# A two-block network on one core: convolutions of the later tiles behind the first solve, in ten row buffers; a tenth expert weight buffer

## The chip, the core and the metric

The kernel runs on one core of a Trainium2 chip. The core has a matmul engine (TensorE, PE in the rows; its weight loads are PEld), an elementwise engine (VectorE, DVE), an activation engine (ScalarE, ACT), GpSimd (POOL) and a queue engine that mostly starts transfers (SyncE, SP). Each executes its own list of instructions in order, and they wait for each other by semaphores. TensorE writes into eight banks of PSUM; everything else lies in SBUF, 128 partitions wide. The metric is the device time of one execution in microseconds.

## The reference, cut to what matters

512 tokens of width 1024 pass through two blocks. The change touches the first one and the seam between them.

```python
# first block
h   = layer_norm(x)
proj = h @ w_in + b_in                       # u,v | q,k,v | z | a,b | gates
qkv = silu(causal_dwconv(dn_qkv, conv_w))    # 24 channel blocks of 128, 4 taps along time
q, k = q / norm(q), k / norm(k)              # per head, 8 heads of 128
amat = I + strict_lower(beta * (k k^T) * decay)
sol  = triangular_solve(amat, [v*beta, k*beta*exp(G)])
o    = recurrence over chunks(sol, q, k)
h1 = layer_norm(ALPHA * h + mix @ w_o)       # mix: gated v-branch and delta-rule branch
# routed experts: 32, each with w1, w3 (1024 x 512) and w2 (512 x 1024), two per token
h2 = layer_norm(ALPHA * h1 + sum_of_two_experts(h1))
# second block: attention, gated recurrence, feed-forward on 16 + 512 tokens
```

All matmuls of the projections are done in two parts for accuracy: every factor is split into a rounded high part and a low part, and three products are summed.

## The kernel before

**Projections.** Work of the first block comes in "dense tiles" ("d", n): 128 output columns by 512 tokens. TensorE does eight steps (k) of two 512-wide matmuls with the high half of the weights, then eight with the low half (`p_dense`). ScalarE makes the high half ahead of time (`s_split_w`, buffers WHU and WHM), VectorE or GpSimd the low half (`low_split_w`, buffers WL). Tiles 0 to 23 are the q, k and v channels, in the order of the list `ORD`. Each of them goes through `s_evac` (ScalarE copies the tile to a row buffer `xps[n % 3]` in ST and scales it into BG), `v_qkv` (three multiply-adds on VectorE, L267, the convolution) and `s_silu` (SiLU, and for q and k a square for the norm). Four squares make one group `r` of sums: `p_sum(r, y, bank)`, four matmuls one column wide (128x1). The groups follow tiles 3 to 9 (r of 0 and 1) or lie inside tiles 18 and 22 (r of 2 and 3).

**Heads.** Tiles 0 to 11 run first (`p_qk` and its counterparts of the other engines). Then `heads` weaves two things on every engine, by a generator that gives one piece of two heads and one piece of the dense work in turn: `p_head`, `v_head`, `s_head`, `g_head` for heads in pairs, and `p_dense1`, `v_dense1`, `s_dense1`, `g_dense1` for tiles 12 to 71. So the order on each engine is fixed by where the `yield`s stand, and an engine that waits in one of the two stands still for both. A head begins with products k k^T and q k^T, masked on VectorE (`LT`, `AT`), then comes the solve of its 16-wide diagonal blocks, for both heads of a pair at once, row by row on VectorE (`v_sub_rows`, L1066 and the tensor-tensor operations around it, `v_sub_spread` last). TensorE then turns the result (tile ("x0", h), L281), and three levels of products complete the inverse (tiles y, xt and xx, with a subtraction on VectorE). At the end of a head its output is scaled by a norm in the next pair's time (`v_tail_sums`, `s_tail` for the root, `v_tail_spread`, `p_tail_scale`, `v_tail`).

**Beta.** `p_beta`, `s_beta` put the scaled betas in rows, SP stores them and spreads them over all partitions (KB); heads can't begin without.

**Experts.** 96 weights of 2 MB go in order into nine buffers (`EXP_SLOTS`); SP starts a load when the buffer's last reader is done (`w_used`) and, for the first round, when what lay in the region has been read (`w_room`). The region H holds h1, 4 x 1024 columns on 128 partitions, all through the experts; it is stored to DRAM (`h1d`) before, from where GpSimd gathers the experts' rows. In `v_meta` VectorE multiplies H by ALPHA, and `p_rows_h` adds it to the result with an identity matrix.

## Time and profile before

| | us |
|---|---|
| median of three runs | 2147.68 (2144.34 to 2149.09) |
| profiled execution, its own time | 2143.43 |
| span of the profile | 2141.5 |
| TensorE busy | 1966.6 |
| VectorE, ScalarE, GpSimd busy | 931.1, 665.3, 443.6 |

The span is the time from the first to the last recorded instruction of one profiled execution; its own time has some 2 us of start and end besides. A row of a timeline has the start, the length, the engine, the line, the operation, what is written and read, and in brackets how long the engine stood idle before it and who released it. "x3" means three instructions in one row, as long as from the first start to the last end. In a row of stretches the granted clock is a share of full speed, 1.00 for 2.4 GHz and 0.50 for 1.2 GHz. A square-sum `p_sum` shows as 128x1 x8.

### The profile page before, as it was taken

The page shows a single profiled execution, that of the slowest core. Times are in us where ns is not written, and L with a number is a line of the kernel's source. Part 1 is how long each engine was busy: PE and PEld are TensorE (multiplying, and loading weights), DVE is VectorE, ACT ScalarE, POOL GpSimd, SP SyncE. Part 2 cuts the span into 40 slices and gives each one's busy share as a digit, 9 for nine tenths or more (in the row PEclk, how much of TensorE's full clock was granted, in tenths as well). Part 3 has the DMA queues.
Part 4 walks back from the last instruction along what each step waited for, and adds up shares of the span by engine and source line. Part 5 has one row for each costly group of instructions (what it writes and reads, how often), then busy time and mean ns, then how long its engine had stood idle before and what let it go on. Part 6 is the DMA issues. An engine that isn't in the chain of part 4 may idle for free.

```text
span 2141.5 us, 23001 instructions
## 1 busy us (share of the span) xinstructions
PE 1966.6 (92%) x9509; PEld 1434.1 (67%) x9509; DVE 931.1 (43%) x1402; ACT 665.3 (31%) x990; POOL 443.6 (21%) x310
## 2 busy tenths in 40 slices
PE   7989999999999889878878799998889999999999
PEld 6768878888777733333333348777667787888887
DVE  6775476643536622111111145445545883222342
ACT  4553432524333101000000133451237753222221
POOL 5542231423325011111111021311003210000121
PEclk9998999999999889999899999999999999999999
DMA  4873443133334589999999963211111134323211
GB/s 166 265 180 69 99 79 79 43 96 79 69 132 177 208 330 409 402 406 409 409 406 411 424 249 122 86 50 50 50 50 40 40 128 157 118 79 113 85 59 40
DMA packets 107782, 367.37 MB, mean 172 GB/s; under 512 B 10666, under 2 KB 43692, under 8 KB 95384
## 3 DMA queue, kind: packets, MB, share of 16 engines
q1 hardware_dynamic: 96928, 341.49, 45.3%
q0 software_dynamic: 8240, 19.00, 2.6%
q10 hardware_dynamic: 2504, 5.35, 0.7%
q8 instruction: 78, 1.28, 0.2%
q14 instruction: 32, 0.26, 0.0%
HBM read 342.94 MB, written 29.15 MB: 174 GB/s over the span
## 4 chain that ended last, share of the span: by engine, by line
PE 77%; DVE 12%; issue 5%; ACT 4%; DMA 1%; POOL 1%; ACTq 0%; SPq 0%; DVEq 0%; POOLq 0%
PE ps L277 72%; PE ps L281 3%; DVE ST L261 2%; PE ps L2151 2%; DVE H L267 1%; ACT ST L273 1%; ACT L273 1%; DVE BG L267 1%; DVE ST L1066 1%; DVE WL L261 1%; ACT M L273 1%; DVE BG L261 0%; DVE ST L1048 0%; DVE ML L261 0%; DVE H L264 0%
## 5 line engine op out<-in xcount | busy, mean ns | idle before, releaser
L277 PE MATMUL ps<-XH,WS 128*128 128x512 f32 x704 | 216.9, 389 | 0.0
L277 PE MATMUL ps<-W,BG 128*64 128x512 f32 x496 | 160.8, 619 | 1.0 <-issue 1.0
L277 PEld LDWEIGHTS ps<-XH,WS 128*128 128x128 f32 x704 | 132.2, 188 | 27.5
L2258 DVE COPY BG<-ps 128x512 f32<-128x512 f32 x32 | 22.1, 692 | 288.0 <-PE ps L277 288.0
L271 ACT ACTIVATE BG<-ps 128x512 f32<-128x512 f32 x48 | 28.6, 595 | 374.9 <-PE ps L2151 339.2
L277 PE MATMUL ps<-XL,WS 128*128 128x512 f32 x352 | 137.0, 389 | 1.4 <-DVE XL L261 1.4
L277 PE MATMUL ps<-X2H,GV 128*128 128x512 f32 (+1 forms) x512 | 127.8, 340 | 0.0
L277 PE MATMUL ps<-M,BG 128*64 128x512 f32 (+1 forms) x304 | 121.6, 544 | 6.4 <-ACT ST L271 6.4
L277 PE MATMUL ps<-ST,BG 128*64 128x512 f32 (+2 forms) x416 | 101.5, 589 | 25.4 <-issue 22.6
L277 PE MATMUL ps<-HTH,WL 128*128 128x512 f32 x448 | 115.1, 394 | 1.4 <-DVE WL L261 1.4
L277 PE MATMUL ps<-BG 128*64 128x512 f32 (+2 forms) x256 | 93.0, 544 | 20.8 <-issue 20.8
L277 PE MATMUL ps<-WS,HH 128*128 128x512 f32 x352 | 108.4, 389 | 0.9 <-DVE WS L261 0.9
L277 PE MATMUL ps<-U,BG 128*64 128x512 f32 x176 | 84.9, 639 | 21.2 <-issue 21.2
L261 POOL TENSOR_TENSOR WS<-W,WS 128x1024 fp32r<-128x1024 f32 x11 | 26.4, 2397 | 362.6 <-ACT WS L271 362.6
L277 PEld LDWEIGHTS ps<-HTH,WL 128*128 128x128 f32 x448 | 85.3, 191 | 20.7 <-DVE WL L261 2.1
L273 ACT ACT_TABLE_LOAD x71 | 91.1, 1283 | 19.6 <-PE ps L277 14.1
L277 PEld LDWEIGHTS ps<-X2H,GV 128*128 128x128 f32 x512 | 88.1, 189 | 10.7
L277 PE MATMUL ps<-X2L,GV 128*128 128x512 f32 (+1 forms) x256 | 87.1, 358 | 6.7 <-DVE H L267 5.4
L261 DVE TENSOR_TENSOR BG<-ps,ST 128x512 f32<-128x512 f32 x22 | 15.2, 692 | 179.1 <-PE ps L277 179.1
L277 PEld LDWEIGHTS ps<-ST,BG 128*64 128x64 f32 (+1 forms) x416 | 40.7, 159 | 77.8 <-issue 74.1
L267 DVE SCALAR_TENSOR_TENSOR BG<-ST,pc,BG 128x512 f32<-128x512 f32 x72 | 73.6, 1023 | 42.7 <-ACT BG L271 40.9
L277 PEld LDWEIGHTS ps<-ST 128*128 128x128 f32 x672 | 85.6, 193 | 7.0 <-DVE ST L261 2.5
(397 smaller groups left out, 4370.5 us busy)
## 6 DMA issues: line engine op xcount, KB each, us to landing
W<-in_w SPq DMA_DIRECT2D x31, 2048.0 KB, 39.3
W<-in_w_in SPq DMA_DIRECT2D x27, 2048.0 KB, 11.0
ST<-in_w SPq DMA_DIRECT2D x21, 2048.0 KB, 35.3
BG<-in_w SPq DMA_DIRECT2D x11, 2048.0 KB, 33.4
U<-in_w SPq DMA_DIRECT2D x11, 2048.0 KB, 32.9
M<-in_w SPq DMA_DIRECT2D x11, 2048.0 KB, 37.9
HT<-in_w SPq DMA_DIRECT2D x11, 2048.0 KB, 39.4
W<-in_w_ffn_in SPq DMA_DIRECT2D x22, 1024.0 KB, 7.7
```

The source lines that it names most:

```text
L261: return E.e.tensor_tensor(o, x, y, op)
L267: return v.e.scalar_tensor_tensor(out=o, in0=x, scalar=c, in1=y, op0=op0, op1=op1)
L271: return s.e.activation(o, x, f, scale=scale)
L273: return s.e.activation(o, x, f, bias=bias, scale=scale)
L277: return p.e.matmul(o, lhsT=l, rhs=r, start=start, stop=stop, skip_group_check=True)
L281: return p.e.transpose(o, x, ident[0:n, 0:n])
L1066: v.e.tensor_reduce(o, z, AX.X, ADD, negate=True).then_inc(v.up())
L2151: z = p.e.transpose(t.at[:, k * BLK:(k + 1) * BLK], xg[j][:, k::8], ident[xg_at[j], xg_at[j]])
L2258: v.e.tensor_copy(hs[j], t.at).then_inc(t.drained)
```

## The change

1. Tiles 14 to 23 get ten row buffers, three in ST and seven in the region H (`HR`), free once h0 is stored; `CONV_AT` names at which tile's turn a convolution is done: those of tiles 14 to 21 in pairs at 19 to 22, so none stands in the first solve.
2. The sums go inside tiles: groups 0 and 1 in tiles 5 and 9 (after k of 1, 3, 5, 7), 2 and 3 in tiles 21 and 23 (3, 5, 7, and 9, which is in the low half).
3. Beta of the first four heads goes to its row after tile 10 instead of 11.
4. The head's scale is done later in the next pair: `v_tail_spread` after the second masks, `v_tail` after the solve's first piece, `p_tail_scale` one piece later.
5. ScalarE splits tile 33 one tile sooner.
6. H becomes the tenth expert buffer; h1 is read back from DRAM behind the last expert weight (`q_h1`), and ALPHA is in the identity that TensorE uses.

```diff
+        Wt += [H.rearrange("p a b -> p (a b)")]
-        EXP_SLOTS = (5, 1, 7, 2, 0, 3, 4, 6, 8)
+        EXP_SLOTS = (5, 1, 7, 2, 0, 3, 4, 6, 8, 9)
...
+        HR = H.rearrange("p i d -> p (i d)")[:, 0:516 * 7]
+        xps += [HR[:, 516 * j:516 * j + 515] for j in range(7)]
+        CONV_AT = {12: [12], 13: [13], 19: [14, 15], 20: [16, 17], 21: [18, 19], 22: [20, 21], 23: [22], 24: [23]}
+
+        def xp_of(n):
+            return n % 3 if n < 12 else (n - 12) % 10
...
+            elif xp_before(n) is None:
+                s.wait_ge(first_done, 3)
             else:
-                s.wait_ge(conv_done, n - 2)
+                s.wait_ge(conv_done, xp_before(n) + 1)
...
-        SUMS_AFTER = {3: [(0, 0)], 4: [(0, 1)], 5: [(0, 2), (0, 3)], 7: [(1, 0)], 8: [(1, 1)], 9: [(1, 2), (1, 3)]}
+        def sums_in(r, bank):
+            return {k: (r, y, bank) for y, k in enumerate((1, 3, 5, 7) if r < 2 else (3, 5, 7, 9))}
...
             tt(v, AT, four(t.at), C, MUL).then_inc(t.drained)
-            if h > 1:
-                v_tail_spread(h - 2)
             yield
...
             v_sub_take(h)
+            if h > 1:
+                v_tail_spread(h - 2)
             yield
-            if h > 1:
-                v_tail(h - 2)
...
                 yield
+                if h > 1 and i0 == 1:
+                    v_tail(h - 2)
...
-                r = {18: 2, 22: 3}.get(n)
+                r = {21: 2, 23: 3}.get(n)
...
-                if n == 30:
-                    s_split_w(32)
+                if n >= 30:
+                    s_split_w(n + 2)
...
-                v_qkv(n)
+                for m in CONV_AT.get(n, ()):
+                    v_qkv(m)
...
-            v.wait_ge(c_h1, 64)
-            for i in range(NT):
-                ts(v, H[:, i, :], H[:, i, :], ALPHA, None, MUL, None).then_inc(alpha_done)
...
-                mm(t.at[:, z], ident, H[:, i, z], stop=False)
+                mm(t.at[:, z], ident_a, H[:, i, z], stop=False)
...
+        def q_h1():
+            for x in w_used[max(n for n in range(N_EXP, N_SEC) if slot[n] == 9)]:
+                q.wait_ge(*x)
+            q.e.dma_start(H, h1d.rearrange("(i p) d -> p i d", p=P)).then_inc(c_h0, 16)
...
+            w_room[N_EXP + EXP_SLOTS.index(9)] = [(c_h1, 64), B["h1", NT - 1, 1].full()]
```

VectorE in the middle of the first pair's solve, before; the operations from ST to ST are rows of the solve, BG<-ST,pc,BG x3 is a tile's convolution.

```order
L261 TENSOR_TENSOR ST<-ST 128x98
L1066 TENSOR_REDUCE ST<-ST 128x2x7
L267 SCALAR_TENSOR_TENSOR BG<-ST,pc,BG 128x512 x3
L261 TENSOR_TENSOR ST<-ST 128x128
L1066 TENSOR_REDUCE ST<-ST 128x2x8
```

And of the change, from the same row of the solve on.

```order
L262 TENSOR_TENSOR ST<-ST 128x98
L1081 TENSOR_REDUCE ST<-ST 128x2x7
L262 TENSOR_TENSOR ST<-ST 128x128
L1081 TENSOR_REDUCE ST<-ST 128x2x8
L262 TENSOR_TENSOR ST<-ST 128x162
L1081 TENSOR_REDUCE ST<-ST 128x2x9
```

Further on in the same list: the last mask of the solve, and what follows it.

```order
L262 TENSOR_TENSOR ST<-lv,ST 128x512
L262 TENSOR_TENSOR WL_52<-W,WHM 128x8x128
L268 SCALAR_TENSOR_TENSOR BG<-ST,pc,BG 128x512 x3
L268 SCALAR_TENSOR_TENSOR BG<-H,pc,BG 128x512 x3
L1300 MEMSET ST 128x8x32
L262 TENSOR_TENSOR ST<-ST,ps 128x16x16
```

The convolutions have left the solve; two of them stand between its last mask and the first level's subtraction, and the second reads its row buffer in H.

TensorE around the end of tile 9, before: the last low half, the row of G, then two sums in one.

```order
L277 MATMUL ps<-HTL,WHU 128x512
L277 MATMUL ps<-HTH,WHU 128x512
L277 MATMUL ps<-HTH,WL_51 128x512 x8
L277 MATMUL ps<-cst,sm 32x128
L277 MATMUL ps<-cst,ST 128x1 x8
```

And of the change, the last two sums of the tile.

```order
L278 MATMUL ps<-cst,ST 128x1 x4
L278 MATMUL ps<-HTL,WHU 128x512
L278 MATMUL ps<-HTH,WHU 128x512
L278 MATMUL ps<-HTL,WHU 128x512
L278 MATMUL ps<-HTH,WHU 128x512
L278 MATMUL ps<-cst,ST 128x1 x4
L278 MATMUL ps<-HTH,WL_51 128x512 x8
L278 MATMUL ps<-cst,sm 32x128
```

All four sums now come ahead of the tile's low half, so the last square is asked for eight matmuls sooner.

SP at the end of the experts' weights, of the change.

```order
L382 DMA HT<-in_w 128x4096
L382 DMA W<-in_w 128x4096
L2662 DMA H<-h1d 128x4x1024
L382 DMA W<-in_w_in 128x8x512 x2
L2667 DMA h0d<-H 128x1024 x4
```

The read of h1 stands between the last expert weight and the second block's first; before, the two loads followed each other directly.

## Rows read from the trace of the kernel before

**Rows 1.** the page, its head and the first part: busy time of TensorE

```profile
span 2141.5 us, 23001 instructions
...
PE 1966.6 (92%) x9509; PEld 1434.1 (67%) x9509; DVE 931.1 (43%) x1402; ACT 665.3 (31%) x990; POOL 443.6 (21%) x310
```

**Rows 2.** stretches: span, TensorE's busy time, granted clock, DMA share, GB/s

```profile
115.00:640.00 525.00, 499.06 (x2708) 0.97 0.38 92
...
760.00:1250.00 490.00, 420.19 (x1924) 0.93 0.99 399
1250.00:2142.00 892.00, 848.46 (x3954) 0.99 0.25 85
```

**Rows 3.** timeline of TensorE; start, length, instructions, [idle before <-releaser]

```profile
95.03 1.87 PE L277 MATMUL ps<-cst,ST 128*128 128x1 f32 x8 [1.54 <-ACT ST L273]
...
123.04 1.16 PE L277 MATMUL ps<-ST,BG 128*128 128x128 f32 x8 [1.74 <-DVE ST L261]
...
157.83 1.87 PE L277 MATMUL ps<-cst,M 128*128 128x1 f32 x8 [6.60 <-ACT BG L271]
...
160.56 1.70 PE L277 MATMUL ps<-cst,M 128*128 128x1 f32 x8
...
174.05 1.04 PE L281 MATMUL ps<-cst,ST 128*128 128x128 f32 x8
```

**Rows 4.** timeline of VectorE through the first solve

```profile
131.48 2.33 DVE L267 SCALAR_TENSOR_TENSOR BG<-ST,pc,BG 128x512 f32<-128x512 f32 x3 [4.84 <-ACT BG L271]
...
139.75 5.09 DVE L267 SCALAR_TENSOR_TENSOR BG<-ST,pc,BG 128x512 f32<-128x512 f32 x3
...
148.07 2.41 DVE L261 TENSOR_TENSOR ST<-ST 128x50 f32<-128x50 f32 x1
...
172.61 0.92 DVE L261 TENSOR_TENSOR ST<-lv,ST 128x512 f32<-128x512 bf16 x1
...
183.92 2.33 DVE L267 SCALAR_TENSOR_TENSOR BG<-ST,pc,BG 128x512 f32<-128x512 f32 x3 [6.21 <-ACT BG L271]
```

**Rows 5.** timeline of GpSimd at 147 us

```profile
147.20 3.21 POOL L261 TENSOR_TENSOR WL<-W,WHU 128x1024 fp32r<-128x1024 f32 x1 [2.91 <-ACT WHU L271]
```

**Rows 6.** timeline of TensorE from 205 us, and the stretch from 210 us

```profile
205.68 0.95 PE L277 MATMUL ps<-cst,M 128*128 128x1 f32 x8
...
211.56 3.38 PE L277 MATMUL ps<-HTH,WL 128*128 128x512 f32 x8
...
222.01 2.00 PE L277 MATMUL ps<-HTH,WL 128*128 128x512 f32 x8
...
210.00:220.00 10.00, 10.00 (x47) 0.77 0.00 0
```

**Rows 7.** timelines of ScalarE and TensorE, second pair of heads

```profile
295.38 1.06 ACT L271 ACTIVATE WHU<-W 128x1024 fp32r<-128x1024 f32 x1 [1.59 <-issue]
...
296.58 0.77 PE L277 MATMUL ps<-HTL,WHU 128*128 128x512 f32 x1 [3.72 <-ACT WHU L271]
```

**Rows 8.** timelines of VectorE and TensorE, third and fourth pair

```profile
403.16 0.18 DVE L1223 RECIPROCAL sm<-sm 128x4 f32<-128x4 f32 x1 [3.66 <-ACT sm L273]
...
433.98 0.66 PE L281 MATMUL ps<-cst,ST 128*128 128x128 f32 x4 [2.46 <-DVE ST L261]
...
556.93 0.66 PE L281 MATMUL ps<-cst,ST 128*128 128x128 f32 x4 [2.86 <-DVE ST L261]
```

**Rows 9.** stretches of 4 us, and the timeline of SP's queue

```profile
764.00:768.00 4.00, 4.00 (x20) 0.99 0.06 20
...
776.00:780.00 4.00, 4.00 (x24) 1.00 0.99 414
...
756.51 12.14 SPq L381 DMA_DIRECT2D ST<-in_w  x2
```

**Rows 10.** stretch of 4 us at the experts' end, and timeline of ScalarE

```profile
1244.00:1248.00 4.00, 3.80 (x20) 1.00 0.40 157
...
1254.08 1.90 ACT L271 ACTIVATE G<-W 128x2048 fp32r<-128x2048 f32 x1
```

More of the change, by code:

```diff
@@ L354, in build @@
         srcs += [w1024(a["w_ffn_out_2"][0], 4 * n, min(4, 22 - 4 * n)) for n in range(6)]
-        EXP_SLOTS = (5, 1, 7, 2, 0, 3, 4, 6, 8)
+        EXP_SLOTS = (5, 1, 7, 2, 0, 3, 4, 6, 8, 9)
         EXP_LAST = (5, 7, 3, 4, 6, 1)
         slot = [n % 2 for n in range(18)] + [0, 1, 2, 0]
-        slot += [EXP_SLOTS[n % 9] for n in range(3 * NE - 6)] + list(EXP_LAST)
+        slot += [EXP_SLOTS[n % 10] for n in range(3 * NE - 6)] + list(EXP_LAST)
         slot += [2, 0, 1, 2] + [(0, 1)[n % 2] for n in range(N_FFI - N_SEC - 4)]
         slot += [(2, 1, 0)[n % 3] for n in range(len(srcs) - N_FFI)]
-        w_sem = [sem(f"weights{i}_loaded") for i in range(9)]
-        w_ready, w_count = [], [0] * 9
+        w_sem = [sem(f"weights{i}_loaded") for i in range(10)]
+        w_ready, w_count = [], [0] * 10
         for n, i in enumerate(slot):
@@ L684, in p_dense @@
                     z = mm(t.at, lo[:, k, :], rhs[0][:, k, :], start=False, stop=k == 7)
+                    if 8 + k in between:
+                        p_sum(*between[8 + k])
             z.then_inc(t.filled)
@@ L718, in build, with xp_before @@
         xps = [XP[:, 516 * j:516 * j + 515] for j in range(3)]
+        HR = H.rearrange("p i d -> p (i d)")[:, 0:516 * 7]
[3 more added lines that the diff above has]
+            return n % 3 if n < 12 else (n - 12) % 10
+        def xp_before(n):
+            return max((m for m in range(n) if xp_of(m) == xp_of(n)), default=None)
         def s_evac(n):
-            t, x = B["d", n], xps[n % 3]
+            t, x = B["d", n], xps[xp_of(n)]
             s.wait_ge(*t.full())
@@ L933, in p_qk @@
             for n in range(12):
-                for _ in first[n] if n < 2 else p_dense(n, n % 4, hTp, "T"):
+                between = sums_in(n // 9, 6 + n // 9) if n in (5, 9) else ()
+                for _ in first[n] if n < 2 else p_dense(n, n % 4, hTp, "T", between):
                     pass
@@ L942, in p_qk @@
                 elif n == 10:
+                    p_beta(1, 6)
                     p_prep3()
-                for r, y in SUMS_AFTER.get(n, ()):
-                    p_sum(r, y, 6 + r)
-            p_beta(1, 6)
         def s_qk():
@@ L973, in v_qk @@
                     v_ab()
+                if n == 10:
+                    v_sums(1)
                 v_qkv(n)
@@ L1128, in p_head @@
                 p_tail_sums(h - 2)
-            yield
-            yield
-            yield
+            for _ in range(4):
+                yield
             if h > 1:
                 p_tail_scale(h - 2)
-            for _ in range(8):
+            for _ in range(7):
                 yield
@@ L1413, in p_dense1 @@
             for n in range(12, 24):
-                r = {18: 2, 22: 3}.get(n)
-                yield from p_dense(n, n % 2, hTp, "T", {k: (r, k - 1, 1) for k in range(1, 5)} if r else ())
+                r = {21: 2, 23: 3}.get(n)
+                yield from p_dense(n, n % 2, hTp, "T", sums_in(r, 0) if r else ())
                 yield
@@ L1509, in s_dense1 @@
                 yield
-                if n == 22:
+                if n == 23:
                     s_sums(3)
                 s_evac(n)
-                s_silu(n - 1)
+                for m in [11] if n == 12 else CONV_AT.get(n - 1, ()):
+                    s_silu(m)
                 yield
-            s_silu(23)
-            s.wait_ge(conv_done, 24)
-            s_row(1, a["gm_ln_g"][0])
-            s_row(2, a["gm_ln_b"][0])
             for n in range(24, 32):
+                if n == 26:
+                    s.wait_ge(conv_done, 24)
+                    s_row(1, a["gm_ln_g"][0])
+                    s_row(2, a["gm_ln_b"][0])
                 if n == 26:
@@ L1524, in s_dense1 @@
                 yield
-                if n == 24:
+                if n == 26:
                     s_beta(3)
+                for m in CONV_AT.get(n - 1, ()):
+                    s_silu(m)
                 m, y = n % 4, (n - 24) // 4
@@ L1589, in v_dense1 @@
                 yield
+                for m in CONV_AT.get(n, ()):
+                    v_qkv(m)
                 m, y = n % 4, (n - 24) // 4
@@ L2222, in s_experts @@
                     s.e.dma_start(ST[:, 16:18, :].rearrange("p a b -> p (a b)"), rope_d).then_inc(c_rp, 16)
+                    act(ident_a, ident, ACT.Copy, scale=ALPHA).then_inc(dg_done)
                     s.wait_ge(dst_done, 1)
@@ L3819, in _ @@
             q_merge()
-            for n in range(21, N_SEC + 2):
+            for n in range(21, N_SEC):
+                q_weight(n)
+            q_h1()
+            for n in range(N_SEC, N_SEC + 2):
                 q_weight(n)
```

35 lines of the change are left out of this document (20 added, 15 removed).

## The prediction, made before the changed kernel was run

> **What bounds the kernel now.** I read the page first: TensorE is busy 92% of the span [rows 1]. Next the waits of TensorE and the stretches, to see where the other 8% lies. From 115 to 640 us (the eight heads of the delta rule, woven with the projections) TensorE is busy 499 of 525 us at a mean granted clock of 0.97; from 760 to 1250 us (the experts) it is busy 420 of 490 us, and there the DMA share is 0.99 at 399 GB/s, so the weights' transfers set the pace; behind 1250 us little is lost and nothing is edited but who scales the residual [rows 2]. So a gain must be a wait of TensorE or low clock before 640 us, or bytes moved earlier in the expert stage. The chain that ended last runs through TensorE almost everywhere in the woven stage, and through VectorE in four places: the triangular solves, one for each pair of heads. Third view, the timelines round those.
>
> In the first solve TensorE stands 6.60 us at 157.83, and the four sums of squares in that tile then run at half clock: 1.70 us each [rows 3] against 0.95 us in a later tile [rows 6]. Its releaser is the square on ScalarE, whose convolution on VectorE stood in line between pieces of the solve. VectorE has no gap there: four convolutions (tiles 14 to 17) lie between 139.75 and 172.61 us, the first of 5.09 us, three of the 2.33 us that one takes undisturbed [rows 4].
>
> **The first solve.** In the new order those four follow the solve. VectorE's path gets shorter by 5.09 + 3 x 2.33 = 12.1 us. It also starts earlier: the row sums' product goes to TensorE one tile sooner, so the spread of beta comes earlier and the 1.74 us wait at 123.04 [rows 3] goes; the solve itself cannot start more than about those 1.7 us earlier, since the convolution of tile 13 (131.48, it waited 4.84 us for ScalarE's copy of that tile) still stands ahead of it [rows 4]. The last mask then begins at 172.61 - 12.1 - 1.7 = 158.8 us. TensorE comes there earlier than that: 174.05 less 6.60, less 1.74, less four slow sums of 1.70 and some 4 us of half clock, is about 155, so it waits for the solve; it turns XT at about 159.0 and not at 174.05. **Term: -15.0 us.** The four sums come back in tile 21: 4 x 0.8 (0.95 us, overlapping its neighbours a little) [rows 6]. **Term: +3.2.** Bounds: -7.5, if only half of it shows, and -17, if GpSimd's collisions (below) miss the solve.
>
> **Clock in tiles 21 to 23.** From 210 to 220 us TensorE is granted 0.77, though it never idles: four sums, each behind only two wide matmuls, and then small half products go before it. Eight wide matmuls take 3.38 us at 211.56 and 2.00 at 222.01 [rows 6]. Counting this group and the two before it, 3.2 us. The new sums have four wide matmuls between them (k of 3, 5, 7, 9), and fewer small ones in any stretch. **Term: -3.2** (bounds 0 and -3.2).
>
> **Tiles 5 to 10.** The sums move inside tiles 5 and 9. In tile 9 this is bad: the square of tile 7 is late (TensorE waited 1.54 us for it at 95.03, with the tile done [rows 3]), and TensorE now meets it ahead of eight wide matmuls (2.0 us) and without the sum that stood before it (0.8): a wait of 1.54 + 2.0 + 0.8 = 4.3 us, of which only the low clock behind it, 1.4 us on eight matmuls, is new loss, since the rest is work that still runs. Tile 5's sums no longer stand in one lump, which may spare as much. I take **0** for all of it, bounds -4 and +4.
>
> **Ten row buffers, tiles 19 to 25.** VectorE now does two convolutions in each of tiles 19 to 22, 4.7 us where 2.3 stood, and ScalarE two SiLUs and squares in a row; ahead of the levels' subtractions in both engines' order. What hides them: their inputs lie ready in ten buffers, so VectorE does them while TensorE runs a tile (24 wide matmuls, 6 us at the pace of rows 6, and the heads' products); before, it stood 6.21 us for the copy of tile 18 [rows 4]. SiLU of tile 23 now falls between two GELUs, with table loads. I take **+1.5**; bounds 0 and, with every one of the six subtractions behind a pair of convolutions, 6 x 4.66 = +28.
>
> **Later solves.** Second pair: the split of tile 33 is issued before ScalarE queues two row loads (it waited 1.59 us for that issue at 295.38), and TensorE's 3.72 us at 296.58 shrink [rows 7]; VectorE's solve is right behind as next limit, and it gains the same 1.6 us, and some 0.9 (a quarter of the 3.66 us that the third pair shows) because the head's scale no longer stands ahead of a mask. **Term: -2.5**, bounds 0 and -6. Third and fourth: VectorE stood 3.66 us at 403.16 for ScalarE's root; TensorE waits 2.46 and 2.86 us at the end of those solves [rows 8]. The scale's work moves behind the first sum of the solve, so the second head's masks fill the gap. But only those masks fit in, two operations at a third of 2.33 us, 1.6 us, and the two spreads still have to be done ahead of the solve's end. **Term: -1 each, -2**; bounds 0 and -7.
>
> **The tenth weight buffer.** SP issues the ninth expert weight at 756.51 and the tenth transfer 12 us later, when the first expert has read its weights; from 764 to 768 us the DMA share is 0.06, while from 776 on it is 0.99 at 414 GB/s [rows 9]. H is free by then (its rows are stored and turned), so a transfer of 2.1 MB, 5.1 us at 410 GB/s, fills the hole. As the stage runs at the DMA's pace from then on, its end comes earlier by what the hole held. **Term: -4.8**, bounds 0 and -5.1. By the Trainium skill (DMA: Bandwidth & Descriptors, Bandwidth) a core reads HBM at about 358 GB/s; the trace does not agree, it shows 399 to 414, and at 358 the hole would hold less than one buffer and the term would still be its 4.5 us.
>
> **What comes in.** H must be read back, 2.1 MB, and it goes ahead of the second block's first weight. Before, the DMA had run dry between 1244 and 1248 us (share 0.40) and the first split of that weight began at 1254.08 [rows 10]. With the experts' end 5 us earlier and 5 us of H added, the weight lands at the same 1246, and is needed at 1249: hidden with some 3 us to spare. The scaling by alpha leaves VectorE, which waited for ScalarE there anyway, and moves into TensorE's identity: same matmuls, one small copy. **0**; bounds 0 and +3.
>
> **Sum:** -15.0 + 3.2 - 3.2 + 0 + 1.5 - 2.5 - 2 - 4.8 = -22.8. The span goes from 2141.5 to 2118.7 us. The profiled execution took 2143.4; the runs' median, 2147.7, is 4.3 above it, and the lowest 2144.3. Taken from the median: 2124.9; since the profiled execution was below all three runs I lean a little under that, **2124.0**.
>
> **Collisions on VectorE.** At 148.07 a sum of 50 elements took 2.41 us, and ended with GpSimd's split (147.20, 3.21 us) [rows 4, 5]; the convolution at 139.75 lost 2.76 us the same way. The Trainium skill (SBUF — State Buffer, section Who interferes with whom) says that a VectorE operation with two SBUF inputs and a GpSimd operation that reads SBUF exclude each other for a whole instruction; by that rule, with which these rows agree, the paired convolutions should meet GpSimd's splits more often. That is the third rival's mechanism.
>
> **Rivals.**
> 1. *The later solves open wholly.* All of 3.72, 2.46 and 2.86 us and some 3 us of low clock behind them go, 12 us where I count 4.5: 2116.5. Against it: VectorE is gapless through those solves.
> 2. *The hole in the DMA isn't worth anything*, because the end of the expert stage is set by something else: the row gathers, or the stand at the meta tokens. 2129. Against it: 0.99 share over the stage.
> 3. *Levels behind paired convolutions.* Two or three of the six subtractions wait the whole 4.66: 12 us back, 2136. Should all six be exposed, with one collision of 2.76 us, 28 + 2.8 - 1.5 come in against a gain of 22.8: 2153, slower than before. It decides from five on: five leave 2146, no change. For it: in-order engines, 4.7 us in one lump. Against it: the 6.21 us that VectorE stood idle there.
> 4. *The first solve stays bound elsewhere* (a weight that lands late for ScalarE's split of tile 20, masks of GpSimd): half of the first term, 2131.5.
>
> **Chances.** Forecast 0.50 (its own range 2119 to 2130), rival 1 0.14, rival 2 0.10, rival 3 in part 0.12, with five exposed 0.04 and whole 0.04, rival 4 0.06. Eight in ten: 2112 to 2138. A measurement of this kernel tells about 0.2% (4.3 us) from no change. Faster 0.92, same 0.04, slower 0.04.
>
> **What would show it.** VectorE's solve of the first pair without convolutions, ended near 159; TensorE's 6.60 us idle gone, a short one of 2 to 3 us before the turn; a new idle of some 4 us in tile 9; clock 1.00 where 0.77 stood; DMA share near 1 from 760 to 768, and the last expert 4 to 5 us closer to the first. Wrong would be: idle of TensorE behind subtractions between 160 and 220, or the second block's first split later than TensorE's end of the experts.

## The result, and the profile after

The changed kernel took 2130.99 us in the median of four runs (2129.22 to 2132.55), the kernel before 2148.39 us beside it (four runs, 2144.34 to 2151.56): a ratio of 0.9934, 95% interval 0.992 to 0.9949. Measured once more beside the last kernels below, it had a ratio of 0.995 (0.9932 to 0.9967). The profiled execution took 2129.22 us, its span is 2127.3: 14.2 us less than before. Forecast were 22.8 us less and a time of 2124.0, in a range of 2112 to 2138. So the direction and the range of eight in ten held, but the median lies 7.0 us above the forecast time, just outside the forecast's own range (2119 to 2130), and by the spans 8.6 us of the forecast gain are missing.

The page of the changed kernel, its head and TensorE's busy time (to be held against [rows 1]):

```profile
span 2127.3 us, 23006 instructions
...
PE 1961.0 (92%) x9509; PEld 1428.6 (67%) x9509; DVE 933.9 (44%) x1398; ACT 669.0 (31%) x994; POOL 441.0 (21%) x311
```

The chain and the shares say little here; the timeline does. A "turn" below is TensorE's transpose of a solved block, the row cst,ST 128x128 x8 (the last of them cst,BG). TensorE in the changed kernel, through the first solve and the levels behind it (beside [rows 3, 6]):

```profile
93.55 1.57 PE L278 MATMUL ps<-cst,ST 128*128 128x1 f32 x8 [3.78 <-ACT ST L274]
...
124.21 3.75 PE L278 MATMUL ps<-ST,BG 128*128 128x128 f32 x16 [2.41 <-DVE ST L262]
...
163.88 2.21 PE L282 MATMUL ps<-cst,ST 128*128 128x128 f32 x8 [3.75 <-DVE ST L262]
...
210.84 1.94 PE L282 MATMUL ps<-cst,BG 128*128 128x128 f32 x16
```

The 6.60 us wait at 157.83 is gone, and XT is turned 10.2 us earlier (174.05, now 163.88). But the wait for beta is still there (2.41 us), and a wait of 3.75 us stands ahead of the turn. Stretches of the same kernel (length, then the busy time of TensorE, its weight loads, VectorE, ScalarE and GpSimd, then granted clock, DMA share and GB/s) show what follows those two waits, and that the low clock of [rows 6] is gone:

```profile
120.00:130.00 10.00, 7.59 (x34) 6.34 (x34) 7.79 (x5) 3.81 (x6) 8.57 (x8) 0.83 1.00 233
160.00:170.00 10.00, 6.25 (x21) 4.88 (x21) 7.20 (x10) 1.71 (x3) 0.51 (x1) 0.66 0.00 2
...
210.00:220.00 10.00, 10.00 (x74) 9.28 (x73) 9.19 (x14) 5.62 (x7) 2.47 (x1) 1.00 0.16 25
```

VectorE in the changed kernel (beside [rows 4]), then GpSimd in the same stretch:

```profile
118.79 3.91 DVE L268 SCALAR_TENSOR_TENSOR BG<-ST,pc,BG 128x512 f32<-128x512 f32 x3 [2.07 <-ACT BG L272]
...
122.62 3.21 DVE L262 TENSOR_TENSOR ST<-BG,KB 128x512 f32<-128x512 f32 x2
...
132.29 2.33 DVE L268 SCALAR_TENSOR_TENSOR BG<-ST,pc,BG 128x512 f32<-128x512 f32 x3 [4.47 <-ACT BG L272]
...
139.61 1.04 DVE L1063 TENSOR_REDUCE ST<-ST 128x64 f32<-128x512 f32 x1
...
144.51 2.12 DVE L262 TENSOR_TENSOR ST<-ST 128x32 f32<-128x32 f32 x1
...
158.42 2.81 DVE L262 TENSOR_TENSOR ST<-ST 128x450 f32<-128x450 f32 x1
...
164.03 0.90 DVE L262 TENSOR_TENSOR ST<-lv,ST 128x512 f32<-128x512 bf16 x1
```

```profile
139.01 2.93 POOL L262 TENSOR_TENSOR WL<-W,WHU 128x1024 fp32r<-128x1024 f32 x1
...
144.20 2.38 POOL L262 TENSOR_TENSOR WL<-W,WHU 128x1024 fp32r<-128x1024 f32 x1
...
158.16 2.35 POOL L262 TENSOR_TENSOR WL<-W,WHM 128x1024 fp32r<-128x1024 f32 x1 [11.58 <-ACT WHM L272]
```

The four convolutions are out of the solve. Its last mask begins at 164.03, where 158.8 was forecast: the convolution ahead of the solve began at 132.29 and not before 131.48 as it should, and products of 32 and 450 elements last 2.1 and 2.8 us beside GpSimd's splits, 0.2 and 1.0 us without them (run pool_free below).

The later pairs of heads, TensorE:

```profile
276.29 1.10 PE L278 MATMUL ps<-ST,cst 128*128 128x512 f32 x2 [1.24 <-DVE ST L262]
...
399.78 1.10 PE L278 MATMUL ps<-ST,cst 128*128 128x512 f32 x2 [1.08 <-DVE ST L262]
403.16 1.10 PE L278 MATMUL ps<-ST,cst 128*128 128x512 f32 x2 [2.29 <-DVE ST L262]
...
527.70 2.04 PE L278 MATMUL ps<-ST,cst 128*128 128x512 f32 x2 [2.28 <-DVE ST L262]
...
549.23 1.04 PE L282 MATMUL ps<-cst,ST 128*128 128x128 f32 x8
```

The waits of 2.46 and 2.86 us ahead of the turns [rows 8] are gone. In their place TensorE waits at the product that spreads the output scale: 6.9 us in four rows.

How far the changed kernel is ahead of the kernel before, at the same instruction of TensorE (start before less start after):

| place | before | after | ahead |
|---|---|---|---|
| first turn of XT, pair 1 | 174.05 | 163.88 | 10.2 |
| second turn | 186.86 | 179.14 | 7.7 |
| third turn (four sums came back ahead of it) | 199.77 | 195.47 | 4.3 |
| turn behind the levels | 219.34 | 210.84 | 8.5 |
| turn, pair 2 | 311.71 | 301.37 | 10.3 |
| turn, pair 3 | 433.98 | 425.04 | 8.9 |
| second turn, pair 4 | 570.37 | 561.95 | 8.4 |
| first expert's transposes | 756.49 | 747.94 | 8.6 |
| router turn in the experts' last part | 1228.68 | 1214.01 | 14.7 |
| second block's transposes | 1287.43 | 1273.10 | 14.3 |

### The profile page after: what moved, and what is told of

It reads as the page before. It is cut to its first block, busy times and chain, and to the rows that moved or that the text cites. A ratio compares the mean times of both kernels' runs of the same rounds, so it can differ in the third digit from the quotient of the medians.

```text
span 2127.3 us, 23006 instructions
## 1 busy us (share of the span) xinstructions
PE 1961.0 (92%) x9509; PEld 1428.6 (67%) x9509; DVE 933.9 (44%) x1398; ACT 669.0 (31%) x994; POOL 441.0 (21%) x311
## 4 chain that ended last, share of the span: by engine, by line
PE 77%; DVE 12%; issue 4%; ACT 4%; DMA 2%; POOL 0%; SPq 0%; DVEq 0%; POOLq 0%; ACTq 0%
PE ps L278 72%; PE ps L282 3%; DVE ST L262 3%; DMA W<-in_w_in 2%; PE ps L2176 1%; ACT ST L274 1%; DVE H L268 1%; ACT L274 1%; ACT M L274 1%; DVE ST L1081 1%; DVE WL L262 1%; DVE BG L262 0%; DVE BG L268 0%; DVE ML L262 0%; DVE ST L1063 0%
## 5 line engine op out<-in xcount | busy, mean ns | idle before, releaser
L278 PE MATMUL ps<-ST,BG 128*64 128x512 f32 (+2 forms) x384 | 137.4, 567 | 8.8 <-issue 5.0
L278 PE MATMUL ps<-M,BG 128*64 128x512 f32 (+1 forms) x288 | 105.1, 545 | 11.5 <-ACT ST L272 6.4
L278 PEld LDWEIGHTS ps<-W,BG 128*64 128x64 f32 x448 | 46.8, 144 | 78.4 <-issue 77.4
L278 PEld LDWEIGHTS ps<-X2H,GV 128*128 128x128 f32 x512 | 89.5, 192 | 10.7
L278 PE MATMUL ps<-H,BG 128*64 128x512 f32 (+1 forms) x256 | 84.6, 525 | 12.6 <-issue 8.3
L272 ACT ACTIVATE WS<-W 128x2048 fp32r<-128x2048 f32 (+1 forms) x44 | 65.3, 1484 | 78.1 <-PE ps L278 64.3
L2303 POOL DMA_INDIRECT BG<-h1d,toki x32 | 30.9, 966 | 277.7 <-PE ps L2176 263.1
```

The lines of the kernel that those rows point to most:

```text
L272: return s.e.activation(o, x, f, scale=scale)
L278: return p.e.matmul(o, lhsT=l, rhs=r, start=start, stop=stop, skip_group_check=True)
L2303: g.e.indirect_dma_start(out=xg[j], out_offset=None, in_=h1d, in_offset=bass.IndirectOffsetOnAxis(ap=toki[:, b:b + 1], axis=0), bounds_che ...
```

## The experiments

Up to 1.8 us of a place in time belongs to the execution: the wait of tile 9 ended between 92.91 and 94.67 us in nine profiles of kernels that are the same up to there. Where less than that matters, I count from that row ("from tile 9"), which does not take all of it away: in five profiles with the same order up to there, the fourth turn comes 115.93 to 117.77 us behind it and the first 69.33 to 70.84 us; "the fourth turn" is the row at 210.84. Each run lies beside the kernel before on its chip.

**Undoing the parts.** Without the tenth buffer:

```
-        EXP_SLOTS = (5, 1, 7, 2, 0, 3, 4, 6, 8, 9)
+        EXP_SLOTS = (5, 1, 7, 2, 0, 3, 4, 6, 8)
...
-            q.e.dma_start(H, h1d.rearrange("(i p) d -> p i d", p=P)).then_inc(c_h0, 16)
+            pass
```

> The changed kernel without the tenth weight buffer: nine buffers for the experts, H not overwritten and so not read back; ALPHA stays in TensorE's identity. Up to the first expert it is the changed kernel (first transposes at 747.9 us). My theory: the expert stage and the seam behind it gave 5.8 us of the 14.2 (first transposes 8.55 us earlier than before, second block's first transposes of M 14.33 earlier), all of it by the buffer that fills the hole in the DMA; the span goes from 2127.3 to about 2133.1, and a stretch of 4 us near 756 shows a DMA share near 0.06 again. Rival 1: part of it is the scaling by alpha that left VectorE at the seam; then the span is 2130 to 2131.5. Rival 2: reading H back costs something at the seam, so without it less is lost: 2131.

Measured: 2135.03 us, ratio 0.995 (0.9934 to 0.9966), which is also the ratio of the changed kernel in its second measurement. But the profiled execution, the fastest of the six, has a span of 2128.6, 1.3 us more than the changed kernel's and not 5.8. The first 20 us of the stage (from 4 us ahead of the first transposes), first the changed kernel, then this one:

```profile
743.94:763.94 20.00, 15.23 (x82) 7.39 (x84) 5.17 (x22) 2.86 (x4) 3.70 (x4) 0.78 0.88 321
```

```profile
742.50:762.50 20.00, 15.22 (x82) 7.36 (x84) 5.14 (x22) 2.86 (x4) 3.68 (x4) 0.78 0.71 236
```

The hole is real: 0.17 of 20 us, 3.4 us of all the DMA engines. My 5.8 us for it was wrong for this profile, and the rivals' 2130 to 2131.5 were too high for it as well; the runs' median does not tell them apart. No run put alpha back on VectorE, so the first rival was not tested by itself. More on it at the end of this section.

With each convolution in its own tile again:

```
-        CONV_AT = {12: [12], 13: [13], 19: [14, 15], 20: [16, 17], 21: [18, 19], 22: [20, 21], 23: [22], 24: [23]}
+        CONV_AT = {n: [n] for n in range(12, 24)}
...
-                r = {21: 2, 23: 3}.get(n)
+                r = {18: 2, 22: 3}.get(n)
```

> The changed kernel with each convolution of tiles 14 to 23 in its own tile again, as before, and the sums of squares that depend on them in tiles 18 and 22 again (with the new spacing inside the tile). My theory: VectorE's path through the first solve gets four convolutions back, 5.0 + 3 x 2.24 = 11.7 us, less what of the 5.5 us of collisions with GpSimd moves away; TensorE turns XT at 173 to 176 us in place of 163.9, the half clock behind that wait stays, and the sums no longer stand in tile 21; at the fourth turn behind the first pair (210.84 us now) the lag is 8 to 10 us, the span 2135 to 2137. Rival: the gain came from the sums' spacing and the clock at 200 to 220 us (4.2 us), not from VectorE's path; then the span is 2131 or less.

Measured: 2138.46 us, ratio 0.996 (0.9946 to 0.9973), span 2136.3. TensorE, and the stretch in which its tile 22 runs:

```profile
156.41 1.38 PE L278 MATMUL ps<-cst,M 128*128 128x1 f32 x8 [4.31 <-ACT BG L272]
...
172.35 1.04 PE L282 MATMUL ps<-cst,ST 128*128 128x128 f32 x8
...
198.04 1.03 PE L282 MATMUL ps<-cst,ST 128*128 128x128 f32 x8
...
214.39 1.80 PE L282 MATMUL ps<-cst,BG 128*128 128x128 f32 x15
```

```profile
205.00:215.00 10.00, 10.00 (x66) 8.92 (x66) 3.96 (x9) 6.78 (x9) 0.38 (x1) 1.00 0.00 1
```

Both theories were half right. At the first turn the move of the convolutions (and of the sums that follow them out of tile 18) is worth 8.5 us (172.35 against 163.88), at the fourth only 3.6 (214.39 against 210.84). The other 5.0 us of the 8.5 that the change has there (219.34 less 214.39) are kept by a kernel whose convolutions lie as before. Of these, 1.7 us are there at the first turn already (174.05 less 172.35), where TensorE waits 4.31 us in place of 6.60. The larger part comes later: from the third to the fourth turn TensorE takes 19.57 us before, 16.35 here, 15.37 in the changed kernel. The same four sums of tile 22 stand in this stretch before and here, only with four wide matmuls between the first and second and between the second and third, where there were two; the last two sums still have two between them, which the prediction had as four. Their spacing is worth 3.2 us, and the granted clock there is 1.00 where it was 0.77 [rows 6].

With the output scale in its old places (TensorE's product one step earlier, VectorE's spread behind the mask of AT, its use ahead of the solve's first sum):

```
+            if h > 1:
+                v_tail_spread(h - 2)
             yield
             v.wait_ge(de_done, 2 * h + 2)
...
             v_sub_take(h)
-            if h > 1:
-                v_tail_spread(h - 2)
```

> The changed kernel with the three edits of the output scale undone (VectorE's spread and scale and TensorE's scale product in their old places in each head). The prediction's theory: the later scale spares VectorE about 1 us in each later solve, so this kernel is slower by 2 to 3 us: 2129 to 2130. My theory now: the later scale left TensorE's product in line ahead of it, which waits 1.24 us at 276.29, 1.08 and 2.29 at 399.78 and 403.16, 2.28 at 527.70; undone, those go and the waits before the turns at 425 and 549 us come back with 1 to 2.9 us each, so that it is even or slightly faster: 2125 to 2127.5. The places tell: of the 1.9 us that the changed kernel lost against before between 311 and 570 us, this one loses none.

Measured: 2135.33 us in the median of five runs (a sixth took 7711.94 us and is left out), ratio 0.994 (0.9926 to 0.9955); span 2135.0. TensorE's turns of pair 3 and 4:

```profile
424.16 0.66 PE L282 MATMUL ps<-cst,ST 128*128 128x128 f32 x4 [2.45 <-DVE ST L262]
...
548.76 2.22 PE L282 MATMUL ps<-cst,ST 128*128 128x128 f32 x8 [2.87 <-DVE ST L262]
...
588.56 1.91 PE L282 MATMUL ps<-cst,BG 128*128 128x128 f32 x16
```

The four waits at the scale are gone and the two ahead of the turns are back, as my theory had it. Between the turn of pair 2 and the row at 588.56 this kernel takes 286.65 us (from 301.91), the changed one 286.05 (301.37 to 587.42): level within 0.6 us. But the kernel before took 284.14 us there (311.71 to 595.85), with the same order and the same waits as this run, 2.46 and 2.86 us. The difference of 2.5 us is the clock behind these waits: from the turn to the next one this run takes 15.04 and 14.32 us, the kernel before 13.43 and 13.44. The stretch behind the turn of pair 3, before and in this run:

```profile
433.90:438.90 5.00, 4.47 (x26) 3.73 (x27) 2.86 (x5) 1.72 (x3) 1.71 (x1) 1.00 0.27 72
```

```profile
424.10:429.10 5.00, 4.49 (x16) 3.62 (x17) 2.85 (x5) 1.72 (x3) 1.42 (x1) 0.66 0.72 90
```

So the scale's move costs 1.9 us against an execution in which the clock stays up behind the old waits, and gains 0.6 us against one in which it falls; what decides between the two is not shown. My 2125 to 2127.5 was wrong. The span is 8 us longer, nearly all of it for reasons behind 588 us: 2.6 more up to the experts, 2.4 in them, 2.2 at their end, where nothing is edited.

With tiles 3 to 11 in their old order (beta's product behind tile 11, sums behind tiles 3, 4, 5, 7, 8, 9):

```
-                between = sums_in(n // 9, 6 + n // 9) if n in (5, 9) else ()
...
+                for r, y in SUMS_AFTER.get(n, ()):
+                    p_sum(r, y, 6 + r)
+            p_beta(1, 6)
```

> The changed kernel with the order of tiles 3 to 11 as before (sums of squares of q and k behind tiles 3, 4, 5, 7, 8 and 9, product of beta behind tile 11, the wait for eG ahead of beta). The prediction's theory: beta earlier takes a wait of 1.7 us away and starts the solve as much earlier, the sums cost nothing; so this kernel is 1.7 us slower, 2129. My theory now: the wait ahead of the second products (2.41 us at 124.21 now, 1.74 + 0.30 before) was only handed from the DMA of beta's rows to a convolution of VectorE that stands in line there, and the 3.78 us at 93.55 are new; without both the solve starts 0.8 us earlier and the span is 2126 to 2127.

Measured: 2129.03 us, ratio 0.9917 (0.9904 to 0.9929), span 2130.8. TensorE:

```profile
93.51 1.62 PE L278 MATMUL ps<-cst,ST 128*128 128x1 f32 x8 [1.52 <-ACT ST L274]
...
121.42 1.16 PE L278 MATMUL ps<-ST,BG 128*128 128x128 f32 x8 [1.65 <-DVE ST L262]
...
162.74 2.22 PE L282 MATMUL ps<-cst,ST 128*128 128x128 f32 x8 [3.63 <-DVE ST L262]
```

The wait in tile 9 is 1.52 us, and at beta there are two, 1.65 and 1.64 us, since VectorE here waits for the DMA of beta's rows before each of its two products. The first turn comes 1.1 us earlier than in the changed kernel and the fourth 0.7 us (210.18), which is less than executions differ by. So the new order of these tiles gains nothing that can be seen; by the prediction this run should have been 1.7 us later. The runs go further: the ratio 0.9917 lies below both of the changed kernel's (0.9934 and 0.995) and its interval clear of the second's. No row up to the fourth turn shows where such a gain would come from, and this run's profiled execution is the slowest of its six; that the old order is faster stays possible and open.

**What holds the first solve.** The convolution of tile 12 behind the products of k and beta:

```
-        CONV_AT = {12: [12], 13: [13], 19: [14, 15], ...
+        CONV_AT = {13: [12, 13], 19: [14, 15], ...
```

> The changed kernel with the convolution of tile 12 one tile later (both of 12 and 13 in tile 13), so that in VectorE's order the products of k and beta of the first two heads stand ahead of it. My theory: the rows of beta have landed by 120 to 121 us (issued 114.1, 5.2 to 6.7 us to landing), and the wait of 2.41 us at 124.21 is due to that convolution (118.79, 3.91 us) alone; it goes, with the half clock behind it (3.75 us for 16 products where 2.3 would do), and the first turn of XT comes at 160 to 161 in place of 163.9; VectorE's second convolution is hidden in the 4.47 us that it stands idle ahead of 132.29. Rival: the DMA is what is late; then the wait stays at 1.5 us or more and the turn at 163 or later.

Measured: 2128.08 us, ratio 0.9922 (0.9893 to 0.9952), span 2127.0. VectorE, then TensorE:

```profile
120.14 0.70 DVE L262 TENSOR_TENSOR ST<-BG,KB 128x512 f32<-128x512 f32 x1 [2.83 <-DMA KB<-b_rows]
```

```profile
123.70 1.16 PE L278 MATMUL ps<-ST,BG 128*128 128x128 f32 x8 [0.23 <-DVE ST L262]
...
161.48 0.91 PE L282 MATMUL ps<-cst,ST 128*128 128x128 f32 x4 [4.52 <-DVE ST L262]
```

The 2.41 us became 0.23. From tile 9 the first turn comes 3.5 us earlier (66.81 us behind 94.67, against 70.33 behind 93.55) and the fourth 4.1 us (113.15 against 117.29). VectorE waits 2.83 us for the landing of beta's rows, which is just early enough for TensorE. TensorE now waits 4.52 us for the solve: it was moved earlier by as much as the solve.

The splits of tiles 18 and 20 on VectorE (`x not in (('d', 18), ('d', 20))` added to the list of GpSimd's splits):

> The changed kernel with the splits of tiles 18 and 20 (GpSimd, 144.20 with 2.38 us and 158.16 with 2.35 us) given to VectorE, 1.22 us each. My theory: in the first solve each cost VectorE 1.9 us by holding up one small operation (2.12 us for 32 elements at 144.51, 2.81 us for 450 at 158.42), so in VectorE's own hands they cost 2 x 0.7 less: the turn of XT comes 1.4 us earlier, at 162.5, with TensorE's wait ahead of it 1.4 us shorter. Rival: the slow ones are not due to GpSimd; then they stay above 2 us at the same elements and the turn comes 2.4 us later, at 166.3.

Measured: 2128.82 us, ratio 0.992 (0.9896 to 0.9945), span 2126.0. The product of 32 elements takes 0.21 us (2.12 before the edit), that of 450 elements 0.98 (2.81), and TensorE, with the stretch round it:

```profile
161.76 0.66 PE L282 MATMUL ps<-cst,ST 128*128 128x128 f32 x4 [1.00 <-DVE ST L262]
```

```profile
160.00:170.00 10.00, 8.55 (x50) 7.00 (x49) 8.82 (x11) 2.57 (x6) 2.80 (x2) 1.00 0.02 8
```

The wait ahead of the turn is 1.00 in place of 3.75 us. From tile 9 the first turn is 2.6 us earlier (1.6 to 3.1 against the five profiles of one order) where 1.4 were expected, and the fourth 4.4 us (112.84): behind a wait of 1.00 us the half clock does not follow, and from the first turn to the second 13.43 us pass where 15.26 did, so the low clock there cost 1.8 us. GpSimd's splits held up VectorE more than the work itself costs there.

Both convolutions, 12 and 13, behind the solve, four in tile 19:

```
-        CONV_AT = {12: [12], 13: [13], 19: [14, 15], 20: [16, 17], ...
+        CONV_AT = {19: [12, 13, 14, 15], 20: [16, 17], ...
```

> The changed kernel with the convolutions of tiles 12 and 13 behind the first solve too (tile 19 takes 12 to 15, tile 20 takes 16 and 17). My theory: what starts the solve on VectorE is the convolution of tile 13 (132.29, it waits 4.47 us for ScalarE's copy); without it the masks and sums of the solve start at 129 to 131 and the turn of XT comes at 156 to 158 in place of 163.9, about when TensorE gets there, without its wait of 3.75 us and without the half clock of the ten us behind it. At the fourth turn (210.84 now) 6 to 9 us are kept. Rival 1: GpSimd's masks and the exponentials of ScalarE set the start of the solve, and it moves no further than in the kernel with convolution 12 alone moved (turn 160 to 161). Rival 2: four convolutions in a lump in tile 19, 9.3 us, hold up the first level's subtraction; then 3 to 5 us of it are lost again before 211.

Measured: 2131.97 us, ratio 0.9938 (0.9919 to 0.9956), span 2134.9. VectorE, TensorE, and one stretch:

```profile
161.42 8.50 DVE L268 SCALAR_TENSOR_TENSOR BG<-ST,pc,BG 128x512 f32<-128x512 f32 x9
169.83 2.32 DVE L268 SCALAR_TENSOR_TENSOR BG<-H,pc,BG 128x512 f32<-128x512 f32 x3
```

```profile
158.22 0.65 PE L282 MATMUL ps<-cst,ST 128*128 128x128 f32 x4 [1.48 <-DVE ST L262]
172.76 1.97 PE L282 MATMUL ps<-cst,ST 128*128 128x128 f32 x8 [2.06 <-DVE ST L262]
```

```profile
190.00:200.00 10.00, 10.00 (x37) 8.83 (x36) 4.62 (x9) 1.67 (x3) 1.95 (x2) 0.50 0.01 2
```

Theory and second rival both came true. The first turn begins at 156.14, 7.7 us earlier, so the convolution of tile 13 does set its start. Then the level's subtraction stands behind 10.7 us of convolutions (the first three read ST and the fourth H, since tiles 12 and 13 share the ten buffers), TensorE waits 2.06 us, again 0.59 and 0.88 us for ScalarE's eight passes behind the lump, and runs ten us at half clock. From the second turn to the third, at 198.05, 25.3 us pass where 16.3 did, and at the fourth turn (213.47) it is behind the changed kernel.

**The output scale still later**, two steps in TensorE's order of a head, `for _ in range(4)` becoming `range(6)`, and its use on VectorE behind the solve's third sum:

> The changed kernel with TensorE's product that spreads the output scale two steps later in each head (and VectorE's use of it behind the second sum of the solve). My theory: the four waits ahead of it (1.24 us at 276.29, 1.08 and 2.29 at 399.78 and 403.16, 2.28 at 527.70, 6.9 us together) go, but VectorE's solves set the turns at 301, 425 and 549 us: of the 6.9 us most comes back as longer waits there, except in the fourth pair, where TensorE had no wait left at its turn. Relative to the turn at 301, the turn at 425 keeps its distance within 0.5 us, with a wait of 2 to 3.5 us ahead of it. Rival: TensorE's own order is the limit, and all 6.9 us are kept: the row at 587.42 comes 6 to 7 us earlier.

Measured: 2134.2 us, ratio 0.9954 (0.9938 to 0.997), span 2130.2. TensorE's turns of pairs 2, 3 and 4:

```profile
300.24 0.66 PE L282 MATMUL ps<-cst,ST 128*128 128x128 f32 x4 [2.44 <-DVE ST L262]
...
424.31 2.23 PE L282 MATMUL ps<-cst,ST 128*128 128x128 f32 x8 [2.86 <-DVE ST L262]
...
548.13 0.66 PE L282 MATMUL ps<-cst,ST 128*128 128x128 f32 x4 [2.79 <-DVE ST L262]
```

The four waits at the scale are gone, and 2.4 to 2.9 us stand ahead of each turn, in the fourth pair too, where I had expected some of it to be kept. The turns of pairs 2 and 3 lie 124.07 us apart, 123.67 in the changed kernel. Wherever the scale's product stands, the solve ends when it ends. Behind the waits of 2.44 and 2.86 us the clock fell (0.66 and 0.69 in the next 5 us), behind that of 2.79 us it did not (1.00).

**Mixtures, and the tenth buffer again.** Three edits together (tile 12's convolution later, the two splits on VectorE, tile 9's last sum among the half products):

> The changed kernel with three edits: the convolution of tile 12 behind the products of k and beta (as in the run with that alone), the splits of tiles 18 and 20 on VectorE (as in the run with those alone), and the last sum of squares inside tile 9 moved from behind the eighth pair of wide matmuls to among the half products (position 13), with row sums 1, 3, 5 as they are. My theory: the 3.78 us at 93.55 shrink to 1.5 or less, the 2.41 us at 124.21 to 0.3, the 3.75 us at the first turn to 1 or 2, and half clock follows none of them; the two gains of 4.1 and 4.4 us at the fourth turn share 2.5 us of clock, so the fourth turn comes 6 to 8 us earlier than the changed kernel's 210.84, at 203 to 205, and the ratio to the kernel before is 0.990 to 0.991. Rival: VectorE, with two splits more and the convolution of tile 12 inside, becomes later at the start of the solve; then the fourth turn is at 206 or later.

Measured: 2124.25 us, ratio 0.9916 (0.9893 to 0.9939), span 2118.9; the fourth turn at 202.66, 8.2 us earlier. The waits at beta are 0.70 and 1.64 us (TensorE now gets there before beta's rows do), the one in tile 9 is 2.39 where 1.5 or less was expected, the one ahead of the turn 2.02, with the clock at 1.00 behind it.

The same, with 12 and 13 in tile 18 behind the solve:

```
-        CONV_AT = {12: [12], 13: [13], 19: [14, 15], ...
+        CONV_AT = {18: [12, 13], 19: [14, 15], ...
...
+                ... {1: (1, 0, 7), 3: (1, 1, 7), 5: (1, 2, 7), 13: (1, 3, 7)} if n == 9 ...
```

> As the kernel of the run with the same splits and sum, but with the convolutions of both tiles 12 and 13 in tile 18, right behind the first solve, and 14 and 15 in tile 19 as in the changed kernel: two in a tile, where the run with four in tile 19 had a lump. My theory: what that run lost (9 us between the third and the second turn, of them 5 us of half clock at 190 to 200 us) came from the lump of four convolutions and eight passes of ScalarE behind it; spread over two tiles it stays away, the solve ends at 153 to 156, TensorE comes to the first turn without a wait of over 0.5 us, and the fourth turn is at 200 to 203; ratio to the kernel before 0.989 to 0.990. Rival: not the lump, but TensorE that now comes early to the levels is what waits: then the waits before 200 us come back in the other places, 3 us or more, and the fourth turn is at 205 or later.

Measured: 2124.09 us, ratio 0.9905 (0.9888 to 0.9922), span 2123.8. TensorE:

```profile
155.32 1.04 PE L282 MATMUL ps<-cst,ST 128*128 128x128 f32 x8
168.77 1.21 PE L282 MATMUL ps<-cst,ST 128*128 128x128 f32 x8 [0.59 <-DVE ST L262]
...
200.66 1.94 PE L282 MATMUL ps<-cst,BG 128*128 128x128 f32 x16
```

No wait is left ahead of the first turn, and the fourth is at 200.66, 10.2 us earlier than in the changed kernel. Two convolutions in a tile are hidden but for a wait of 0.59 us, four are not: it was the lump.

> The kernel above without the tenth weight buffer (nine buffers, H not read back). The profiles so far disagree on its worth: first expert's transposes to the combined rows took 466.1, 468.4, 469.5, 468.3, 468.8, 467.8, 465.9 and 469.5 us with the buffer and 472.2 and 469.0 without. My theory: the buffer is worth the 4.8 us of the prediction or less, 2 to 4 us, as the executions of the stage differ by 3 us themselves; here the median is 2 to 4 us longer than that of the kernel with the buffer. Rival: it is worth the 6.2 us that the first pair of profiles showed; then 5 to 7 us longer.

Measured: 2125.12 us, ratio 0.9914 (0.9896 to 0.9932), span 2121.8. That is 1.0 us over its twin with the buffer, where 2 to 4 were expected, and less than this measurement can tell.

> The changed kernel once more, beside the others on the same chip, so that the two mixed kernels have it to be compared with: span 2127 to 2131, ratio 0.992 to 0.995. Its places in time before 700 us repeat within 1.2 us (an offset that is there before 95 us), its stretch through the experts within 3 us.

Measured: 2132.48 us, ratio 0.995 (0.9932 to 0.9967), span 2130.6, fourth turn 211.09. Beside it mix_b is 8.4 us shorter, and 21 us shorter than the kernel before (2145.28): the kernel that beats both.

With 14 profiles the tenth buffer can be read by stage. From the first expert's transposes to the router turn near 1214 us, eleven profiles with the buffer take 468.0 us in the mean (465.9 to 469.5), three without it 470.9 (469.0 to 472.2): 2.9 us less. From there to the second block's transposes eleven take 59.5 us (57.6 to 61.3), three 58.4 (57.6 to 58.9): 1.1 us more. The ranges touch or overlap and there are only three profiles without it, so both differences are rough, the second above all. The first pair of profiles, 14.7 less 8.6 us, had paired a slow execution of this stage with a fast one. GpSimd's last two stores of expert rows, first without the buffer, then with it (the changed kernel again):

```profile
1235.55 0.98 POOL L2264 DMA_INDIRECT ypad<-BG,yrow  x1 [10.13 <-DVE BG L2275]
...
1241.00 0.98 POOL L2264 DMA_INDIRECT ypad<-BG,yrow  x1 [2.44 <-DVE BG L2275]
```

```profile
1235.21 0.98 POOL L2265 DMA_INDIRECT ypad<-BG,yrow  x1 [10.13 <-DVE BG L2276]
...
1241.91 0.98 POOL L2265 DMA_INDIRECT ypad<-BG,yrow  x1 [0.80 <-DMA ypad<-BG,yrow]
```

With the buffer the last store follows 6.70 us behind the one before it and not 5.45, and what released it is a DMA. Ten of the eleven profiles with the buffer have 6.0 to 6.7 us there; the eleventh (old_start) and all three without have 5.4 to 5.5. In the profile above TensorE then waits 1.94 us at 1253.57 for rows gathered from that store; in the changed kernel's first profile, with the same 6.70 us, it does not wait there. H's read is issued at 1211.08, with the next weight behind it, and from 1235 to 1240 us the DMA share is 0.56 with the buffer and 0.16 without. That this read is the cause is argued from the rows; no run had the buffer with the read in another place.

## Why the prediction came out as it did

The forecast was right in direction and range, and partly by luck: 12.1 us of what it counted on did not come, and 3.5 us elsewhere made up for a part. The time that was measured is nearer to that of the fourth rival (2131.5, half of the first solve's term), and half is what the first solve gave, though the runs put it on other causes than the two that this rival named.

- **First solve, -15.0: mis-sized, measured -10.2 at the turn.** The mechanism was right, since the run with the convolutions in their own tiles has the turn 8.5 us later. Two things in its working failed. "It also starts earlier" did not hold: beta's rows were early, but its product on VectorE stood in order behind tile 12's convolution, which itself waited for ScalarE and met GpSimd; kb_first showed it. That is 132.29 where 129.8 was forecast, 2.5 us. And GpSimd's collisions stayed in the solve, with one product of 2.12 us and one of 2.81 us: pool_free gave 2.6 us at the turn. The Trainium skill (SBUF — State Buffer, section Who interferes with whom) says that a VectorE product with two SBUF inputs contends with a GpSimd instruction that reads SBUF, and that a reduction on this chip never does; the trace agrees, since the reduction at 139.61 took its usual 1.04 us beside GpSimd's split of 2.93 us, and the products at 144.51 and 158.42 did not keep theirs.
- **The price of the wait that was forecast.** I wrote that TensorE would wait 2 to 3 us for the solve (my own working, 159.0 less 155, gave 4), and priced nothing behind it. It waited 3.75, the stretch from 160 to 170 was granted 0.66, and the lead fell from 10.2 to 7.7 us by the second turn: 1.8 us of that is the clock, by pool_free, and the rest comes with the second head's half of the turn, which waits for its own mask (0.45 us in the changed kernel's second profile). This is the step that is missing from the sum: -2.5 us of the gain. So the first solve gave 7.7, half of the 15.
- **Sums back, +3.2:** measured 3.4 (7.7 to 4.3). Right.
- **Clock in tiles 21 to 23, -3.2:** measured -4.2 up to the row at 210.84, behind which two of tile 23's four sums still come; with the convolutions in their old places and all four sums inside, 3.2. Right, and its cause is the spacing.
- **Tiles 5 to 10, 0:** the wait at 93.55 is 3.78 us, 4.3 were forecast, and old_start is 0.7 us ahead at the fourth turn (by its ratio perhaps more). Right within its bounds.
- **Paired convolutions, +1.5:** no wait behind them above the 0.71 us at 199.96. The third rival did not come, but both_later shows that it was near: four in one tile cost 9 us.
- **Second pair, -2.5:** measured -1.8 (8.5 to 10.3). TensorE's 3.72 us for the split became 0.80, with 1.24 at the scale and 1.67 at the turn in its place. No run undid the earlier split, so its share is read from the rows alone.
- **Third and fourth pair, -2: wrong.** By the table they gave back 1.9 us. Against old_tail the scale's move is level within 0.6 us, but only because that execution lost 2.5 us of clock behind its two waits, which the kernel before did not. The step "the second head's masks fill the gap" left out that TensorE's product stands in order too and moved by one step only; but scale_later shows that this wait is not what bounds the pair, since without it the solve is the limit.
- **Tenth buffer, -4.8, and its price, 0: mis-sized.** By stage -2.9 and +1.1, -1.8 together, and 1.0 by the medians of the twins. The hole held 3.4 us, and the way out seems not to be free: "some 3 us to spare" looked at the weight, not at GpSimd's last stores and gathers, which come later with the buffer. That H's read delays them is argued, not shown. The 4.5 us that the prediction gives for the hole at 358 GB/s is worked out nowhere; the sum used 4.8.

The 8.6 us between the forecast's 22.8 and the measured 14.2 are then: 4.8 at the first turn, 2.5 behind it, 0.2 in the sums, 0.7 in pair 2 and 3.9 in pairs 3 and 4 on the one side, 1.0 in tiles 21 to 23, 1.5 for the pairs of convolutions and 1.0 in the expert stage of this one pair of profiles on the other.

## What to carry over

When a stall is removed, ask which wait TensorE meets next, and count low clock behind it as a bound: here 3.75 us cost another 2.5, of them 1.8 of clock, while behind waits of 2.3 to 2.9 us the clock fell in some profiles and stayed up in others. A wait's releaser in the trace is the last one to come; a second one just behind it (here a convolution in VectorE's order) can keep all of it. And what a DMA-paced stage gains can't be read from one pair of profiles when its executions differ by 3.7 us; twins on one chip, and stages read over many profiles, can.

## What was not expected of the hardware

Here a split of 1.22 us on VectorE was cheaper than the same split on GpSimd beside a chain of small VectorE products: each of GpSimd's two held one product for 1.8 to 1.9 us. Small sums spread with mostly four wide matmuls between them left TensorE at a granted clock of 1.00, with two between them at 0.77, with no idle time in either. And behind a wait of 3.75 us the clock fell to its lower level (a stretch of ten us at 0.66), behind 1.00 us it did not (1.00 in the same stretch). Between these the length of the wait does not tell: in the 5 us behind it the clock was 0.66 to 0.69 after waits of 2.30 (no_tenth), 2.45 and 2.87 (old_tail), 2.44 and 2.86 us (scale_later), and 1.00 after 2.02 (mix_a), 2.46 and 2.86 (before) and 2.79 us (scale_later).
